# Eight start addresses for one split activation tensor in SBUF, and the embedding rows moved into the shared area

## What is computed

```python
for i in range(2):
    hn = rms_norm(h, pre_mix_g[i])
    y = conformer_conv(hn, ...) if i == 0 else diff_attention(hn, ...)
    h = h + rms_norm(y, post_mix_g[i])
    f = conv_ffn(rms_norm(h, pre_ffn_g[i]), ffn_w_in[i], ffn_w_dw[i], ffn_w_out[i])
    h = h + rms_norm(f, post_ffn_g[i])
    gate = sigmoid(rms_norm(h, ple_pre_g[i]) @ ple_w_gate[i] + ple_b_gate[i])
    h = h + rms_norm(gate * (p[i] @ ple_w_proj[i]), ple_post_g[i])
```

## Time and profile before

| | us |
|---|---|
| median of 3 runs | 2512.14 |
| lowest and highest | 2510.94, 2512.44 |
| the profiled execution, its own time | 2504.14 |
| its span, first to last instruction | 2502.3 |
| TensorE busy in it | 2430.5 (97%) |
| VectorE busy | 1666.5 (67%) |
| ScalarE busy | 1307.0 (52%) |
| GpSimd busy | 27.6 (1%) |
| DMA | 179 GB/s mean |

### The profile page before, as it was taken

How to read it: one execution, slowest core, us unless ns; L and a number is a source line. 1 busy time by engine, 2 the same in 40 slices (tenths; PEclk the granted TensorE clock), 3 DMA queues, 4 the chain that set the end, 5 groups by cost and what they waited for, 6 DMA issues and landing times.

```text
span 2502.3 us, 40724 instructions
## 1 busy us (share of the span) xinstructions
PE 2430.5 (97%) x12610; PEld 2082.6 (83%) x12610; DVE 1666.5 (67%) x2183; ACT 1307.0 (52%) x1882; POOL 27.6 (1%) x49
## 2 busy tenths in 40 slices
PE   7999899999999999999999999999999999999997
PEld 6888787888888888887788887888888888888876
DVE  5889756777777764446665577567777777544465
ACT  6555545555555544446454455465655656444463
POOL 1000000000000000000000000000000000000000
PEclk9999999999999999999999999999999999999999
DMA  6444254666566665555565543646666666655554
GB/s 212 133 133 135 76 192 153 193 186 188 183 190 194 192 202 194 193 193 200 183 181 188 189 155 128 203 148 191 194 192 187 185 185 198 204 193 194 194 197 138
DMA packets 365325, 448.28 MB, mean 179 GB/s; under 512 B 27084, under 2 KB 273726, under 8 KB 364076
## 3 DMA queue, kind: packets, MB, share of 16 engines
q1 hardware_dynamic: 363452, 436.75, 54.7%
q0 software_dynamic: 1776, 10.41, 1.3%
HBM read 444.95 MB, written 2.10 MB: 179 GB/s over the span
## 4 chain that ended last, share of the span: by engine, by line
PE 88%; issue 5%; DVE 3%; ACT 2%; DMA 1%; DVEq 0%; SPq 0%; POOL 0%; ACTq 0%; POOLq 0%
PE ps L1273 34%; PE ps L1275 17%; PE ps L1308 11%; PE ps L1310 11%; PE ps L1309 11%; PE ps L1346 2%; PE ps L1253 1%; DVE v_conv L935 1%; DMA gain<-in_post_ffn_g 1%; DVE w_lo L808 1%; PE ps L1412 0%; PE ps L1426 0%; DVE h L860 0%; ACT w_hi L503 0%; DVE x L843 0%
## 5 line engine op out<-in xcount | busy, mean ns | idle before, releaser
L808 DVE TENSOR_TENSOR w_lo<-raw,w_hi 128x1024 fp32r<-128x1024 f32 x824 | 1002.4, 1224 | 664.5 <-ACT w_hi L503 635.7
L1273 PE MATMUL ps<-x,w_hi 128*128 128x512 f32 x3840 | 1341.2, 394 | 7.0 <-DVE w_lo L808 3.8
L503 ACT CAST w_hi<-raw 128x1024 fp32r<-128x1024 f32 x824 | 859.4, 1049 | 839.7 <-PE ps L1275 423.4
L1275 PE MATMUL ps<-x,w_lo 128*128 128x256 f32 x3840 | 1073.7, 280 | 0.0
L1273 PEld LDWEIGHTS ps<-x,w_hi 128*128 128x128 f32 x3840 | 718.9, 187 | 169.8 <-DVE w_lo L808 5.0
L1275 PEld LDWEIGHTS ps<-x,w_lo 128*128 128x128 f32 x3840 | 724.9, 189 | 0.6
L1308 PE MATMUL ps<-w_hi,mid 128*128 128x512 f32 x704 | 274.1, 389 | 4.6 <-DVE w_lo L808 4.6
L1310 PE MATMUL ps<-w_hi,mid 128*128 128x512 f32 x704 | 273.9, 389 | 0.0
L1309 PE MATMUL ps<-w_lo,mid 128*128 128x512 f32 x704 | 273.9, 389 | 0.0
L1308 PE MATMUL ps<-w_hi,x 128*128 128x512 f32 x640 | 254.3, 397 | 7.0 <-DVE x L980 3.6
L1309 PE MATMUL ps<-w_lo,x 128*128 128x512 f32 x640 | 250.1, 391 | 0.0
(11 more groups left out here) (144 smaller groups left out, 1213.9 us busy)
## 6 DMA issues: line engine op xcount, KB each, us to landing
raw<-in_ffn_w_in SPq DMA_DIRECT2D x704, 256.0 KB, 3.1
raw<-in_ffn_w_out SPq DMA_DIRECT2D x352, 256.0 KB, 3.0
raw<-in_conv_w_pw SPq DMA_DIRECT2D x192, 256.0 KB, 3.1
raw<-in_attn_w_qkv SPq DMA_DIRECT2D x192, 256.0 KB, 2.9
raw<-in_ple_w_gate SPq DMA_DIRECT2D x128, 256.0 KB, 3.5
raw<-in_attn_w_o SPq DMA_DIRECT2D x64, 256.0 KB, 3.2
raw<-in_ple_w_proj SPq DMA_DIRECT2D x16, 256.0 KB, 3.4
h<-in_x SPq DMA_DIRECT2D x4, 512.0 KB, 5.9
```

What stands on the lines that cost most here:

```text
L503: nc.scalar.copy(w_hi[:, u % RING], raw[:, u % RING]).then_inc(hi_split, 1)
L808: nc.vector.tensor_tensor(w_lo[:, u % RING], raw[:, u % RING], w_hi[:, u % RING].bitcast(F32), ALU.subtract).then_inc(split_done, 1)
L1273: mm(ps[:, 4 * s + f], w_hi[:, u % RING, q, columns], x[:, kt].rearrange("p a t -> p (a t)"), start=kt == 0, stop=False)
L1275: ins = mm(ps[:, 4 * s + f, 0:T], w_lo[:, u % RING, q, columns], x[:, kt, 0], start=False, stop=kt == KT - 1)
```

## The change

`x` is no longer one tensor. Room for it and 512 bytes more is set aside (`x_at`), and eight tensors of the same shape are laid over each other in it, each starting at its own distance from `x_at`. `x_at` is where `x` stood. All distances are multiples of 32 bytes and under 512. Writers and readers take the tensor of their stage. `p_rows` goes from its own place into the arena, half a slot behind `h_sink`, and the wait for `p_turned` ahead of its second load is gone. The rings therefore stand 512 bytes further (`w_hi` at 172672, `w_lo` at 189056), `p_x` 1536 bytes nearer, and keep their distance of multiples of 512 from `mid` and from `x_at`.

```diff
-    x = sb("x", [P, KT, 2, T], F32R)
+    x_at = top[0]
+    top[0] += 4 * KT * 2 * T + 512
     raw = sb("raw", [P, RING, UNIT_KT, UNIT_N])
     w_hi = sb("w_hi", [P, RING, UNIT_KT, UNIT_N], F32R)
     w_lo = sb("w_lo", [P, RING, UNIT_KT, UNIT_N], F32R)
     ident = sb("ident", [P, P])
     ones = sb("ones", [P, P])
-    p_rows = sb("p_rows", [P, HALVES, PLE])
     p_x = sb("p_x", [P, PLE // P, 2, T], F32R)
...
+    X_SHIFT = {"mix0": 64, "ln": 128, "ffn0": 256, "ple0": 192, "mix1": 320, "attn": 32, "ffn1": 384, "ple1": 448}
+    x = {left: tenant(x_at + shift, f"x_{left}", [P, KT, 2, T], F32R) for left, shift in X_SHIFT.items()}
...
+    p_rows = tenant(arena + 20 * SLOT + SLOT // 2, "p_rows", [P, HALVES, PLE])
...
                 if layer + 1 < DEPTH:
-                    pool.wait_ge(p_turned, layer + 1)
                     pool.dma_start(p_rows[:], rows_of_p(layer + 1)).then_inc(p_landed, 16)
...
-                    nc.scalar.activation(x[:, kt, 0], tiles[:, kt], ACT.Copy, scale=scale(kt)).then_inc(x_hi, 1)
+                    nc.scalar.activation(x[left][:, kt, 0], tiles[:, kt], ACT.Copy, scale=scale(kt)).then_inc(x_hi, 1)
...
-                            mm(ps[:, 4 * s + f], w_hi[:, u % RING, q, columns], x[:, kt].rearrange("p a t -> p (a t)"),
+                            mm(ps[:, 4 * s + f], w_hi[:, u % RING, q, columns], x[left][:, kt].rearrange("p a t -> p (a t)"),
                                start=kt == 0, stop=False)
-                            ins = mm(ps[:, 4 * s + f, 0:T], w_lo[:, u % RING, q, columns], x[:, kt, 0],
+                            ins = mm(ps[:, 4 * s + f, 0:T], w_lo[:, u % RING, q, columns], x[left][:, kt, 0],
                                      start=False, stop=kt == KT - 1)
...
-                    token_unit(u, bank, (2 * j, 2 * j + 1), x, j == 0, j == UPC - 1)
+                    token_unit(u, bank, (2 * j, 2 * j + 1), x[left], j == 0, j == UPC - 1)
```

More of the change, by code:

```diff
@@ L611, in _ @@
                 act.wait_ge(silu_ln, 2 * g + 2)
-                nc.scalar.copy(x[:, 2 * g:2 * g + 2, 0], v_conv[:, 2 * g:2 * g + 2]).then_inc(x_hi, 2)
+                nc.scalar.copy(x["ln"][:, 2 * g:2 * g + 2, 0], v_conv[:, 2 * g:2 * g + 2]).then_inc(x_hi, 2)
             def token_stage(name, add, biases=False, done=0):
@@ L842, in x_low @@
                         dve.wait_ge(x_hi, KT * LEFT[left] + kt + 2)
[L843 removed]
+                    nc.vector.scalar_tensor_tensor(x[left][:, kt, 1], tiles[:, kt], scale(kt), x[left][:, kt, 0].bitcast(F32),
                                                    ALU.mult, ALU.subtract).then_inc(x_ready, 1)
@@ L979, in _ @@
                     dve.wait_ge(x_hi, KT * LEFT["ln"] + 2 * (g - 1))
-                    nc.vector.tensor_tensor(x[:, tiles_of, 1], v_conv[:, tiles_of], x[:, tiles_of, 0].bitcast(F32),
+                    nc.vector.tensor_tensor(x["ln"][:, tiles_of, 1], v_conv[:, tiles_of], x["ln"][:, tiles_of, 0].bitcast(F32),
                                             ALU.subtract).then_inc(x_ready, 2)
@@ L1313, in token_unit, with token_chunk @@
                 ins.then_inc(units_used, 1)
-            def token_chunk(i, first, bank, left=None, between=lambda j: None, start_with=4):
+            def token_chunk(i, first, bank, left, between=lambda j: None, start_with=None):
                 for j in range(UPC):
                     u = first + j
-                    if left is not None:
+                    if start_with is not None:
                         pe.wait_ge(x_ready, KT * LEFT[left] + max(2 * j + 2, start_with))
                     pe.wait_ge(split_done, plus(i, UPC, is_split(u)))
-                    token_unit(u, bank, (2 * j, 2 * j + 1), x, j == 0, j == UPC - 1)
+                    token_unit(u, bank, (2 * j, 2 * j + 1), x[left], j == 0, j == UPC - 1)
                     between(j)
@@ L1406, in v_units @@
                             token_unit(place["v"] + n, lambda half: ps[:, 2 * (c % 2) + half],
-                                       (2 * j, 2 * j + 1), x, j == 0, j == UPC - 1)
+                                       (2 * j, 2 * j + 1), x["mix1"], j == 0, j == UPC - 1)
                     def weighted_sum(b, bank):
@@ L1458, in rest_of_o @@
                             turn(PIECES, range(3, 4))
-                    token_chunk(None, place["wo"], lambda half: ps[:, half], "attn", rest_of_o)
+                    token_chunk(None, place["wo"], lambda half: ps[:, half], "attn", rest_of_o, 4)
                     with pe.Fori(0, NC - 1) as i:
-                        token_chunk(i, place["wo"] + UPC, lambda half: ps[:, (i + 1) * HALVES + half])
+                        token_chunk(i, place["wo"] + UPC, lambda half: ps[:, (i + 1) * HALVES + half], "attn")
                 turn_h(f"mix{layer}", range(NC // 2))
@@ L1495, in _ @@
                 token_chunk(None, place[f"gate{layer}"], lambda half: ps[:, half], f"ple{layer}",
-                            lambda j: turn_h(f"ffn{layer}", range(NC // 2, NC)) if j == 1 else None)
+                            lambda j: turn_h(f"ffn{layer}", range(NC // 2, NC)) if j == 1 else None, 4)
                 for c in range(NC):
@@ L1504, in _ @@
                 with pe.Fori(0, NC - 1) as i:
-                    token_chunk(i, place[f"gates{layer}"], lambda half: ps[:, (i + 1) * HALVES + half])
+                    token_chunk(i, place[f"gates{layer}"], lambda half: ps[:, (i + 1) * HALVES + half], f"ple{layer}")
 _INS = ["x", "p", "pre_mix_g", "post_mix_g", "conv_w_pw1", "conv_b_pw1", "conv_w_dw", "conv_b_dw", "conv_ln_g",
```

## The result

| | before | changed |
|---|---|---|
| median of 3 runs, us | 2512.14 | 2525.30 |
| lowest, highest | 2510.94, 2512.44 | 2524.50, 2526.39 |
| profiled execution: its time, span | 2504.14, 2502.3 | 2526.39, 2524.5 |
| mean granted clock in it | 0.993 | 0.990 |

The account below looks back on a forecast made before the run. The prediction took TensorE's matmul pace to bound the kernel. The shift, the writers and `p_rows` each counted zero, so the median stayed at 2512.1 us (profiled execution 2504.1), with a range of 2430 to 2534.

Parts of the forecast that it names:

- What bounds the kernel: Whole kernel: TensorE is busy 97% of the span, so only a changed pace of its matmuls shows up in full.
- the bounds of the shift: Moving `x` in all eight stages: a gain of at most 104 us, zero, or a loss up to 22 us.
- I take zero: Matmuls on `x`: the forecast chose no effect from the shift, staying at 346.7 ns a pair and 226.7 a token matmul.
- no address bit from 512 upward matters: Read from `down0` and `down1`: the 512 bytes by which the rings move cost nothing.
- an operand far off the grid is neither faster nor much slower: Read from the convolution's plain float32 matmuls at starts 4 bytes apart: 221 and 216 ns, against 216 on the grid.
- the surplus: One-pass matmuls in `up0` and `down0`: 13.3 ns, 32 clock periods, above the columns for each matmul.
- The argument against a clash: A clash from equal positions should vanish once one stream is a period behind, not recur 32 times in each load.
- the rhythm: Rival, chance 0.14: new addresses throw `up0`, `up1` or `qk` into a slower pace, 353.3 ns a pair; 2521 to 2534 us.
- the start itself costs: Rival, chance 0.07: one-pass operands off the grid need more reads; one period more for every matmul would be 4 us.
- The clash is one of position, and the shift ends it: Rival, chance 0.28: shifting `x` ends the surplus in some or all eight stages, 2408 to 2500 us.
- Writers, `p_rows`, the dropped wait: ScalarE's and VectorE's writes of `x`, and the second `p_rows` load without its wait: each forecast at zero.

## Why the prediction was wrong, by its own steps

*What bounds the kernel* was right, and so was how to read it: the whole difference sits in TensorE's start-to-start times, and the other engines are unchanged.

*The step that failed* is the choice between the bounds of the shift: "I take zero". In its place the runs showed 13.2 and 15.2 us more, 16 to 18 by the paces, all of it with the distances. It rested on two readings. The first, that no address bit from 512 upward matters, held: with all distances 0 the rings stood 512 bytes further (and `p_rows` elsewhere), and the ratio was 1.0007. The second did not: "an operand far off the grid is neither faster nor much slower", read from the convolution's plain float32 matmuls, was said to bound the loss well. It bounded nothing for the one-pass form. Those matmuls take 216 ns for 256 columns, two periods a column; that this leaves slack which covers the same effect is the likely reason, and was not tried. In the one-pass form the same offset costs up to 7.4 ns a token matmul and 6.6 a pair at multiples of 16 bytes, and 13.2 a pair at 4 bytes. The bound should have been called unknown on the loss side as on the gain side. Nor was the surplus "the same in all stages": the earlier trace rows already had 353.3 ns in `glu`.

*The argument against a clash* ("should vanish once one stream has been pushed a period behind") came to a conclusion that held, that nothing is to be gained, but it did so by taking the surplus to be independent of place, and it is not: the two streams that start together on the grid are in the best place that was found, not in the worst. Of twelve other distances (ten for pairs) none was under 226.7 or 346.7 ns.

*The rivals.* The measured 2525.3 us lies in the stated range, 2430 to 2534, and even in the 2521 to 2534 of "the rhythm". That is luck: that rival has a long stage at 353.3 ns whatever its distance, while `up1` went to 351.1 with its distance, `up0` stayed, and 14.4 of the 18.2 us come from `up1` and the token stages. The loss is nearest to "the start itself costs", for which I gave 0.07 and one to three periods a matmul. Where it costs a token matmul, the change's distances measured 5 periods (228.9 against 226.9 ns) to 16 (233.3). It isn't a matter of the start of `x` alone either, since 16, 32 and 160 cost a pair nothing, and moving the rings or `mid` costs as moving `x` does. "The rhythm" exists, but not where it would decide: it was seen in `glu` and `qk`, with more than two paces, and is worth about 3 us a stage. Over all profiles `up0` and `up1` on the grid or 256 bytes off it, 14 stages, stood at 346.7 to 346.8 each time. "The clash is one of position, and the shift ends it" had 0.28: position it is, the sign was wrong.

*The Trainium skill* (TensorE: Matmul & The Clock Gate, Step-by-step) has the load and the moving stream on independent ports. By that, as the prediction read it, the distance could have no effect, and it has: 226.7 against 233.3 ns for `mid` alone. The measurement decides. The other citation (the Trainium skill, SBUF — State Buffer, Specifications) has lines of 16 bytes and a penalty for each new line. For the pairs the trace agrees in part: a start inside a line was the dearest, 359.9 ns at 4 bytes. For the token matmuls it was not, 232.4 at 4 against 233.3 at 32. And multiples of 16 are not alike, as 346.7 at 16 and 353.3 at 192 show for the pairs.

*Writers, `p_rows`, the dropped wait*: zero, as forecast. The second load of `p_rows` in the changed kernel is issued at 1162.9 us for a use at 1678.5, and loads of `p_rows` land within 6.8 us.

*What stays open* is the mechanism of the surplus, of its 13.3 ns on the grid too. The runs show that it follows the distance of the operands modulo 256 bytes at the distances tried, differently for the two forms, and that halving every third load made it larger (226.7 to 229.8 ns). It was not tried whether both operands moved together keep their pace, nor which part of TensorE or of SBUF makes the streams wait.

## What to carry to other kernels

Read matmul pace from start to start and compare it with the column count: it shows a few nanoseconds a matmul that a recorded duration hides. In the one-pass float32 form keep the stationary and the moving operand a multiple of 256 bytes apart, unless a measured pace says that another distance is as good, and don't place a tensor at some other offset to fit it in: with 64 bytes on `mid` the kernel took 12.5 us more here. And a bound taken from an operation at half the rate did not hold for the same access at full rate.

## What the runs showed of the hardware that was not expected

At half the clock the surplus is gone. Between some stages TensorE is granted 1.2 GHz for a few microseconds; the changed kernel's timeline at the start of `up1`:

```profile
1661.68 0.63 PE L1276 MATMUL ps<-x_ffn,w_hi 128*128 128x512 f32 x1
...
1664.24 0.63 PE L1276 MATMUL ps<-x_ffn,w_hi 128*128 128x512 f32 x1
```

Four pairs take 2.56 us, 640 ns each, which is exactly 768 columns at 1.2 GHz, at the very distance (384) that costs 31 ns over the columns at 2.4 GHz. At 4 bytes, the dearest distance, the pairs at 1.2 GHz in `up1` took 640 ns too. That suggests, and does not show, that what is waited for has its own time, short enough for half the rate.

Four of the paces are whole multiples of 16 clock periods: 226.7 ns is 544 periods at 2.4 GHz, 233.3 is 560, 346.7 is 832, 353.3 is 848. The others are not; they are means of uneven steps that repeat, such as 226, 229, 232 for the 228.9 of `gates0`. And identical programs can differ by a rhythm that lasts a whole stage (`qk` at 353.1 and at 349.5, and on the grid at 347 and 353). With 512 pairs and 6 ns that is at most 3 us of the 9 between 2505.87 and 2514.67 over 19 runs.
